# A two-block model on one core: the Fourier layer's second transform over half of the positions, with weights shifted by one row

## What is computed

```python
def fourier_branch(hmod, w_in, w_out):
    b, n, _ = hmod.shape
    u, z = jnp.split(hmod @ w_in, 2, axis=-1)
    ug = u.astype(jnp.float32).reshape(b, n, FOURIER_GROUPS, FOURIER_GROUP_DIM)
    f = jnp.fft.fft2(ug, axes=(1, 3), norm='ortho').real
    y = f.reshape(b, n, D_INNER).astype(hmod.dtype) * jax.nn.silu(z)
    return y @ w_out
```

## Time and profile before

| | us |
|---|---|
| median of 3 runs | 1251.84 (1251.54 to 1254.7) |
| profiled execution, device time | 1251.66 |
| its span | 1249.9 |
| PE busy | 1190.5 (95%) |
| DVE busy | 866.0 (69%) |
| ACT busy | 603.1 (48%) |
| POOL busy | 153.4 (12%) |
| mean granted clock of TensorE | 0.985 |
| Fourier stage on PE | 546.2 to 582.4 |
| fout stage on PE | 583.2 to 626.9 |

### The profile page before, as it was taken

One profiled execution on the slowest core, in us unless ns is written; L12 is line 12 of the kernel. 1 busy time (PEld: TensorE's weight loads), 2 busy tenths in 40 slices (PEclk: granted clock), 3 DMA queues, 4 the chain that ended last, 5 costly groups with the idle time before them and its releaser, 6 DMA issues.

```text
span 1249.9 us, 22840 instructions
## 1 busy us (share of the span) xinstructions
PE 1190.5 (95%) x9282; PEld 1109.1 (89%) x9282; DVE 866.0 (69%) x1404; ACT 603.1 (48%) x933; POOL 153.4 (12%) x127
## 2 busy tenths in 40 slices
PE   6999999999999999989999999999989789999996
PEld 3777889888889999989999899999979778999996
DVE  5795974568788677644488787674579977876644
ACT  4432744476665455632353544453455656444433
POOL 0000000000000000002001412210008950222000
PEclk8999999999999999999999999999989899999998
DMA  9847321323222455530544355555433214554550
GB/s 388 333 188 273 132 68 68 135 101 136 101 102 102 149 214 192 195 106 6 198 169 169 135 173 197 183 187 182 156 136 127 77 68 145 193 196 174 190 182 34
DMA packets 27620, 195.59 MB, mean 156 GB/s; under 512 B 3208, under 2 KB 3472, under 8 KB 4112
## 3 DMA queue, kind: packets, MB, share of 16 engines
q1 hardware_dynamic: 26496, 191.90, 42.2%
q10 hardware_dynamic: 1040, 2.50, 0.6%
HBM read 193.33 MB, written 1.05 MB: 156 GB/s over the span
## 4 chain that ended last, share of the span: by engine, by line
PE 83%; DVE 9%; ACT 4%; DMA 3%; issue 1%; SPq 0%; POOL 0%; ACTq 0%; DVEq 0%
PE ps L450 24%; PE ps L451 24%; PE ps L452 24%; DVE acc L2301 3%; PE ps L800 2%; PE ps L475 2%; DVE w_lo L1658 2%; DMA ada_room<-in_weights 1%; DMA ring<-in_weights 1%; PE ps L493 1%; PE ps L787 1%; PE ps L622 1%; ACT x_hi L1377 1%; ACT w_hi L1076 1%; PE ps L843 1%
## 5 line engine op out<-in xcount | busy, mean ns | idle before, releaser
L1658 DVE TENSOR_TENSOR w_lo<-ring,w_hi 128x1024 fp32r<-128x1024 f32 x282 | 349.9, 1259 | 173.6 <-ACT w_hi L1076 166.4
L1076 ACT ACTIVATE w_hi<-ring 128x1024 fp32r<-128x1024 f32 x300 | 311.1, 1054 | 301.5 <-PE ps L452 218.2
L450 PE MATMUL ps<-x_hi,w_hi 128*128 128x258 f32 (+1 forms) x1216 | 346.2, 285 | 7.6 <-DVE x_lo L2032 4.1
L451 PE MATMUL ps<-x_lo,w_hi 128*128 128x258 f32 (+1 forms) x1216 | 343.7, 283 | 0.0
L452 PE MATMUL ps<-x_hi,w_lo 128*128 128x258 f32 (+1 forms) x1216 | 343.3, 282 | 0.0
L450 PEld LDWEIGHTS ps<-x_hi,w_hi 128*128 128x128 f32 x1216 | 230.6, 190 | 11.0 <-issue 10.8
L451 PEld LDWEIGHTS ps<-x_lo,w_hi 128*128 128x128 f32 x1216 | 230.9, 190 | 0.1
L452 PEld LDWEIGHTS ps<-x_hi,w_lo 128*128 128x128 f32 x1216 | 230.5, 190 | 0.0
L450 PE MATMUL ps<-g_hi,w_hi 128*128 128x256 f32 x608 | 171.1, 281 | 3.2 <-POOL g_lo L1602 1.7
L452 PE MATMUL ps<-g_hi,w_lo 128*128 128x256 f32 x608 | 170.4, 280 | 0.0
L451 PE MATMUL ps<-g_lo,w_hi 128*128 128x256 f32 x608 | 170.4, 280 | 0.0
(11 more groups left out here) (356 smaller groups left out, 1933.4 us busy)
## 6 DMA issues: line engine op xcount, KB each, us to landing
ring<-in_weights SPq DMA_DIRECT2D x156, 1024.0 KB, 4.8
o_sb<-in_weights SPq DMA_DIRECT2D x10, 1024.0 KB, 7.5
ada_room<-in_weights SPq DMA_DIRECT2D x10, 1024.0 KB, 8.3
V<-in_weights SPq DMA_DIRECT2D x3, 1024.0 KB, 24.3
dft<-in_dft ACTq DMA_DIRECT2D x1, 1026.0 KB, 7.3
X<-in_x SPq DMA_DIRECT2D x1, 1024.0 KB, 5.0
xconv<-in_ctx SPq DMA_DIRECT2D x1, 1024.0 KB, 7.5
xconv<-in_weights SPq DMA_DIRECT2D x1, 1024.0 KB, 27.4
```

What stands on the lines that cost most here:

```text
L450: mm(dst, w_h, x_h, start=start, stop=False, skip_group_check=True)
L451: mm(dst, w_h, x_l, start=False, stop=False, skip_group_check=True)
L1076: do(w_hi[:, q % 2, part], ring[:, q % RING, part], ACT.Copy).then_inc(S("hi_ready"), 1)
L1658: v.tensor_tensor(w_lo[:, q % 2, part], ring[:, q % RING, part], w_hi[:, q % 2, part], ALU.subtract).then_inc(S("lo_ready"), 1)
```

## The change

`positions(g)` now computes positions 0 to 129 only (129 for an even count), for both signs in one chain: the weights are `pq` of channels 0 to 127, and the moving operand has two parts of 130 columns, the cosines twice and the sines with either sign. So part s = 0 holds channel p in partition p and part s = 1 holds channel 256 - p. Partition 0 of part 1 would be channel 0 again; channel 128 is put there by six matmuls with one weight column and 130 columns. The positions 129 to 255 are read backwards from the other part by the multiplication on DVE, which becomes two instructions, and a third for partition 0, which takes its own part.

Channel order is now 256 - p instead of 255 - p, one further. Gate columns are shifted while they are rounded: in fin slots 8 to 15 each half's rounding on ACT and its remainder on DVE become three instructions (128 + 127 + 1 columns in each of four blocks). The gates of partition 0 that the third multiplication reads are written apart by two more ACT instructions per slot (`gate_row`). The weight rows of fout are shifted while they are loaded: each of the eight slots is fetched by three transfers, the first half in one, the second half as rows 0 to 126 into partitions 1 to 127, and row 127 into partition 0. ACT waits for a second semaphore, `turned_loaded`, before it rounds either half.

```diff
+        turned_loaded = [S(f"turned_rows_loaded_{s}") for s in range(RING)]
+        def gate_row(g):
+
+            home = (pad_a, gated)[g // 4][0:1].rearrange("p a b -> p (a b)")[:, 2 * P * (g % 4):2 * P * (g % 4 + 1)]
+            return home.rearrange("p (b j) -> p b j", b=2)[:, :, 0:SEQ - DFT_H]
+
+        def mirrored(dst, src, same=False):
+
+            to, of = [a.rearrange("p (k c) -> p k c", c=2 * P) for a in (dst, src)]
+            pairs = []
+            for a, z, at in ((0, P, 0), (P + 1, 2 * P, P), (P, P + 1, 2 * P - 1)):
+                pairs.append((to[:, :, a:z], to[:, :, a:z] if same else of[:, :, at:at + z - a]))
+            return pairs
...
+            def load_mirrored(q):
+
+                s, half = q % RING, SLOT // 2
+                sp.wait_ge(S("lo_ready"), 2 * (q - RING) + 2)
+                src = w_in[block_of(q)]
+                sp.dma_start(ring[:, s, 0:half], src[:, 0:half]).then_inc(loaded[s], 16)
+                sp.dma_start(ring[1:P, s, half:SLOT], src[0:P - 1, half:SLOT]).then_inc(turned_loaded[s], 16)
+                sp.dma_start(ring[0:1, s, half:SLOT], src[P - 1:P, half:SLOT]).then_inc(turned_loaded[s], 16)
...
-            load_rest(STARTS["mout"], turned.start)
+            load_rest(STARTS["mout"], STARTS["fout"])
+            for q in range(STARTS["fout"], STARTS["evin"]):
+                load_mirrored(q)
+            load_rest(STARTS["evin"], turned.start)
...
-                for c in range(2):
-                    for n in range(2):
-
-                        for q, col in ((0, 0), (1, 2 * SEQ if c == 0 else SEQ)):
-                            last = triple(ps[:, 4 + g % 4, c * SEQ:(c + 1) * SEQ],
-                                          [a[:, g % 2, n, q * DFT_H + c:q * DFT_H + c + P] for a in pq],
-                                          [a[:, n, DFT_C + col:DFT_C + col + SEQ] for a in dft_parts],
-                                          c == 0 and n == 0 and q == 0, n == 1 and q == 1)
+                dst = ps[:, 4 + g % 4, 0:2 * DFT_P].rearrange("p (s j) -> p s j", s=2)
+                for n in range(2):
+                    cosines = [a[:, n, DFT_C:DFT_C + DFT_P].rearrange("p (o j) -> p o j", o=1)
+                               .to_broadcast([P, 2, DFT_P]) for a in dft_parts]
+                    sines = [a[:, n, DFT_C + SEQ:DFT_C + 3 * SEQ].rearrange("p (s j) -> p s j", s=2)[:, ::-1, 0:DFT_P]
+                             for a in dft_parts]
+                    triple(dst, [a[:, g % 2, n, 0:P] for a in pq], cosines, n == 0, False)
+                    triple(dst, [a[:, g % 2, n, DFT_H:DFT_H + P] for a in pq], sines, False, n == 1)
+                for n in range(2):
+                    last = triple(ps[0:1, 4 + g % 4, DFT_P:2 * DFT_P], [a[:, g % 2, n, P:P + 1] for a in pq],
+                                  [a[:, n, DFT_C:DFT_C + DFT_P] for a in dft_parts], n == 0, n == 1)
                 last.then_inc(S("f_done"), 1)
...
+                if isinstance(q, int) and STARTS["fout"] <= q < STARTS["evin"]:
+                    act.wait_ge(turned_loaded[q % RING], 32 * ((q - STARTS["fout"]) // RING + 1))
...
+                if t >= 8:
+                    chain.step(last)
+                    for b in range(2):
+                        last = do(gate_row(t - 8)[:, b, :], product[t % 2][0:1, b, DFT_H:], ACT.Silu,
+                                  bias=shift_of[0:1, u, b:b + 1])
...
-                v.tensor_tensor(a, ps[:, 4 + g % 4, :].rearrange("p (c j) -> p c j", c=2), a, ALU.mult)\
+                f = ps[:, 4 + g % 4, 0:2 * DFT_P].rearrange("p (s j) -> p s j", s=2)
+                chain.step(v.tensor_tensor(a[:, :, DFT_H:], f[:, ::-1, DFT_H - 2:0:-1], a[:, :, DFT_H:], ALU.mult))
+                chain.step(v.tensor_tensor(a[:, :, 0:DFT_H], f[:, :, 0:DFT_H], a[:, :, 0:DFT_H], ALU.mult))
+                chain.join(1)
+                v.tensor_tensor(a[0:1, :, DFT_H:], f[0:1, :, DFT_H - 2:0:-1], gate_row(g), ALU.mult)\
                     .then_inc(S("f_moved"), 1)
```

More of the change, by code:

```diff
@@ L44 @@
 DFT_C = 2 * DFT_H
+DFT_P = DFT_H + 1
 UNROLL = 4
@@ L1075, in hi @@
                     part = slice(half * SLOT // 2, (half + 1) * SLOT // 2)
+                    if isinstance(q, int) and STARTS["fin"] + N_FIN // 2 <= q < STARTS["fout"]:
+                        for dst, src in mirrored(w_hi[:, q % 2, part], ring[:, q % RING, part]):
+                            last = do(dst, src, ACT.Copy)
+                        last.then_inc(S("hi_ready"), 1)
+                        continue
                     do(w_hi[:, q % 2, part], ring[:, q % RING, part], ACT.Copy).then_inc(S("hi_ready"), 1)
@@ L1657, in lo @@
                     part = slice(half * SLOT // 2, (half + 1) * SLOT // 2)
+                    if isinstance(q, int) and STARTS["fin"] + N_FIN // 2 <= q < STARTS["fout"]:
+                        hi = w_hi[:, q % 2, part]
+                        for (dst, src), (_, high) in zip(mirrored(w_lo[:, q % 2, part], ring[:, q % RING, part]),
+                                                         mirrored(hi, ring[:, q % RING, part], True)):
+                            last = v.tensor_tensor(dst, src, high, ALU.subtract)
+                        last.then_inc(S("lo_ready"), 1)
+                        continue
                     v.tensor_tensor(w_lo[:, q % 2, part], ring[:, q % RING, part], w_hi[:, q % 2, part],
```

## The result

The changed kernel takes 1348.41 us (median of four runs, 1346.53 to 1350.53) where the kernel before takes 1251.78: a ratio of 1.0753 [1.0735, 1.0772]. The profiled execution took 1346.53 us, 94.9 more than the profiled one of before. The forecast was 1341 in a range from 1326 to 1385, with 0.86 on slower. The measured time lies in the range, and the mechanism is the one that the forecast named.

The account below looks back on a forecast made before the run. TensorE, busy 95%, was taken as the bound; one engine carrying 127 rows would end fout 88.4 us later, edits 1 to 3 included, plus 1 at the norm: 1251.7 + 89.4 = 1341, range 1326 to 1385.

Parts of the forecast that it names:

- Rival B: fout transfers: one engine alone is slower than as one of sixteen, 58 us a block, 1632 us in all; chance 0.03.
- Rival A: fout transfers: the 127 rows are spread over engines, no transfer wait, -5.0 us, 1247 (1243 to 1254); chance 0.12.
- Rival C: Rows spread, but short matmuls cost 0.110 or more and ACT's lag is at its upper bound: 1251 us; chance 0.03.
- Edit 1: Fourier stage, `positions`: 24 matmuls become 12 of 260 and 6 of 130 columns; gain 8.2 us, 6.0 with upper bound.
- Edit 2: DVE product after the transform: one multiplication becomes three, 1.28 us instead of 0.692; +0.6 us in the last group.
- Edit 3: Input map, slots 8 to 15: partition 0's gates and shifted gate columns start the Fourier stage 2.6 us later (0.5 to 5).
- Edit 4: fout weight loads: 127 shifted rows on one DMA engine, 21.3 us a block against 5.75 that PE needs.
- one engine: fout transfers: all 127 rows go to one DMA engine, likeliest 1341 us; chance 0.82, of it 0.77 within 1326 to 1385.

## Why the prediction was right

**The mechanism.** All but one of the marks named ahead were there: DMA slices at 1 tenth, ACT released by the ring's transfers, PE standing for 40.8 us (38 forecast) before the Fourier stage and 13 to 14 before the late slots, the clock at half level after each. The exception is the landing of the shifted rows, 20 to 25 us after their issue by the forecast. The issue for block 6, in SP's queue of the kernel after:

```profile
653.27 0.81 SPq L413 DMA_DIRECT2D ring<-in_weights  x1
```

ACT rounds this block at 688.54, 35 us later. Blocks 1, 5 and 7 take 35 to 36 as well, as each stands behind the block ahead of it; only blocks 0 and 4, with nothing ahead of them, come within 25. The forecast's sum had this queue in it, and only the mark left it out.

The experiments show the mechanism by itself: with the rows spread the loss is gone; with nothing but the 127 rows it is all there; and it follows the divisor of the count. Rival B (1632) is refuted by the plateau of 27 GB/s, the same speed that an engine has as one of sixteen. Rival A came true as soon as the rows were spread. Rival C's high price for the short matmuls is refuted below.

**Edit 1.** The end of `positions` for one group in the kernel after, PE in order of time:

```profile
588.10 0.23 PE L477 MATMUL ps<-dft_parts,pq_hi 128*1 128x130 f32 x1
588.16 0.23 PE L478 MATMUL ps<-dft_parts,pq_hi 128*1 128x130 f32 x1
588.23 0.22 PE L479 MATMUL ps<-dft_parts,pq_lo 128*1 128x130 f32 x1
588.29 0.22 PE L477 MATMUL ps<-dft_parts,pq_hi 128*1 128x130 f32 x1
```

They start 0.062 us apart (0.065 taken): bounded by columns, 0.120 x 130/256 = 0.061. The bounds of 0.110 from unrounded operands and from a full weight load were both far off. A group with its `channels` takes 3.32 us where 4.31 were needed, so 0.99 was won where 1.03 was worked out. Reading the sines' row backwards and the cosines' twice costs nothing that shows.

**Edit 2.** DVE in order of time in the kernel after, one group:

```profile
591.99 0.42 DVE L2202 TENSOR_TENSOR zf<-ps,zf 128x254 f32<-128x254 f32 x1 [0.98 <-PE ps L479]
592.33 0.42 DVE L2203 TENSOR_TENSOR zf<-ps,zf 128x258 f32<-128x258 f32 x1
592.66 0.40 DVE L2205 TENSOR_TENSOR zf<-ps,pad_a 1x254 f32<-1x254 f32 x1
```

Each is near the 0.426 of its bound, but they overlap by 0.08 and so take 1.07 together, not 1.28. In the last group PE starts fout 1.12 us after the product begins (610.48 to 611.60), where it was 0.75 before: +0.4, and +0.6 was priced.

**Edit 3** was mis-sized. A slot's period in slots 8 to 15 is 6.01 us, not 5.75, so ACT falls behind by 0.26 a slot and not by 0.15, and with the rows spread 3.6 us are lost by the seam, not 2.6. The six instructions of a slot's two halves, ACT in order of time in the kernel after:

```profile
512.85 2.36 ACT L1111 ACTIVATE w_hi<-ring 128x512 fp32r<-128x512 f32 x6
...
518.26 0.68 ACT L1451 ACTIVATE pad_a<-sq,shift_of 1x127 f32<-1x127 f32 x2
```

Two roundings of 1024 elements take 2.00 with their overlap, the six take 2.36: 0.18 more a half, where 0.20 was priced. The two gate instructions take 0.59 after overlap (0.68 less 0.09) where 0.5 was priced, and that is most of the 0.11 by which a slot was mis-sized; the rest was not taken apart. In the kernel after the lag is hidden: it only moves the first request of a fout block, to 528.79. As this run lay 1.7 us earlier (366.10 at the common point), that is 3.2 later than before, and 2.7 was forecast.

**Edit 4.** The forecast counted in the times of the kernel before, so the same 1.7 us have to be added to the times after. Then the first fout block landed at 555.7 (553.6 forecast), PE began the Fourier stage at 582.9 (580.4) and fout at 613.3 (609.8), and the last block landed at 712.4 and not at 705.5. Of these 6.9 us, 3.5 were there at fout's start, another 1.9 at block 4 (647.0, where 620.3 + 21.3 = 641.6 was forecast), and 1.6 came in the last three blocks, 65.5 us instead of 63.9. The mis-sized term is mainly the block: 21.6 to 22.2 us instead of 21.3, which was bytes alone. 0.5 is the later request.

Another part is the Fourier stage, which took 30.35 us and not 29.4. After 40.8 us of standing its first 24 matmuls start 0.215 apart, and in the stretch behind the first 3.6 us (clock 0.50) the mean granted clock, third number from the end, is still 0.70:

```profile
584.80:588.00 3.20, 3.20 (x22) 3.20 (x21) 1.14 (x3) 0.77 (x2) 0.00 (x0) 0.70 0.47 154
```

Before, after 4 us of standing, it was 17 matmuls in 3.6 us, and the clock was 1.00 from 550.6 on the earlier trace rows. Seven more at 0.215 instead of 0.12 are 0.7 us, a term that the forecast didn't have.

**A misread row.** The forecast put the end of fout before at 626.9, from DVE's first residual, and set against it the end of the last matmul after. The last matmul of before, and that of after:

```profile
628.73 0.28 PE L452 MATMUL ps<-g_hi,w_lo 128*128 128x256 f32 x1
```

```profile
720.21 0.28 PE L479 MATMUL ps<-g_hi,w_lo 128*128 128x256 f32 x1
```

The first residual begins some 1.9 us before PE is through, as the first bank's sums end earlier; the table of times before has the same early end for fout. Like for like the forecast for this point was 86.5 later, not 88.4. Measured are 91.5, and 93.2 from the common point, so the working was 6.7 us short here. The whole came out only 5.5 short (94.9 against 89.4), and a part of that is luck: the misread row gave back 1.9, and the 1.7 by which the run lay earlier, ahead of all that the change touches, as much again. The last steps were as worked out: 713.11 to 720.3 for 48 matmuls, of it 1.4 for the lower clock (1.6 taken), and 1.2 more until the norm's last instruction (726.14, before 633.44; 1 taken). Another 2.1 of the profiled difference come after that; whether the change makes them is not shown, and the runs scatter by 4.

**The chances** don't add up as put: half of A is 0.06, the rest of A with C 0.09 and one engine with B 0.85, where 0.07, 0.07 and 0.86 stand. Nothing else hangs on that.

## What to carry to other kernels

Before a transfer is cut, factor the row counts: here 127 rows ran on one engine, 122 on two, 124 on four, 125 on five, 120 on fifteen, and an edit that looked like an address shift cost 98 us (1348.41 against 1249.92). Ask of each cut transfer whether its slowest engine still fits in the time that the consumer needs for a block, with an addition per block (0.5 to 1.3 us here) and not by bytes alone. If a fixed reordering of constants can be laid out on the host, do it there. When two ends are compared, compare the same event in both, and from a common point ahead of the change.

## What the runs showed of the hardware that was not expected

To issue a 4 KB transfer behind 127 rows on one engine held SP for 10 to 20 us; behind 61 rows an engine (122 rows) for 3.9 to 6.2 in five of eight blocks and under 0.4 in the others; behind 31 or fewer it took 0.26 to 0.4. With the single row issued first, the next block's issues were held for 4 to 6 us. It looks as if an issue waits for room in the queue of the engine that it needs, but what bounds that queue was not measured. It cost nothing that shows here, as the time was the same when the order of the transfers was exchanged. In a kernel where SP also feeds other buffers, such a hold might delay those; no run here shows that.

One engine alone runs at the same 26 to 27 GB/s as each of sixteen in a burst. And a block costs 0.5 to 1.3 us beyond its rows; which part of the transfer this is stays open.
